# RWKV time mixes on one core: 32x32 blocks instead of 16x16 blocks inverted on VectorE

## Chip, core and metric

The kernel runs on one NeuronCore of a Trainium2 chip. The metric is the device time of one execution in microseconds (us), from the first to the last instruction of the core. A profiled execution gives the trace. Engines are named as in the trace: PE is TensorE (PEld its weight loads), DVE is VectorE, ACT is ScalarE, POOL is GpSimd, SP is SyncE; "ACTq" and the like are instructions by which an engine's queue issues a DMA.

## What is computed

A network of four blocks and a fifth of another kind, for one sequence of 256 tokens, width 1024. Each of the four has a mixer between two feed-forward layers; the mixers are an RWKV-7 time mix, a Mamba-2 mix, a windowed attention and again an RWKV-7 time mix. Only the two time mixes are touched (j = 0 and j = 1 in the code; mix 0 and mix 1 below). Their core, for 16 heads of 64 channels:

```python
def step(state, inp):                      # state 64 x 64 per head
    r_t, w_t, k_t, v_t, kk_t, a_t = inp
    sa = einsum('bhvk,bhk->bhv', state, -kk_t)
    state = (state * w_t[:, :, None, :]
             + sa[..., None] * (kk_t * a_t)[:, :, None, :]
             + v_t[..., None] * k_t[:, :, None, :])
    return state, einsum('bhvk,bhk->bhv', state, r_t)
_, y = lax.scan(step, state0, (r, decay, k, v, kk, a))
y = (y - mean(y)) * rsqrt(var(y) + eps) * ln_w + ln_b      # per head
out = ((y + sum(r * k * r_k) * v) * g) @ w_o
```

r, k, v and the low-rank w, a, g (in mix 1 also the share of the first mix's v, `v_first`) are projections of six mixes of the input with its predecessor.

## The kernel before, in words

The scan over 256 tokens is done in two chunks of 128 (`b`), each for two halves of the heads (`hf`, 8 heads each): four units u = 0 to 3, `RwUnit`. Within a unit the term `sa` needs, per head, the inverse of a unit lower triangular 128 x 128 matrix made of the products of a and kk. It is built up in levels.

**The 16x16 blocks.** While TensorE works on the projections, `near(u)` in `rw_products` multiplies a by kk for all units. ScalarE's `near_read(u)` (L2063) copies the 32x32 diagonal blocks to SBUF, and VectorE's `choose(u)` (L2349) keeps of them the 16x16 blocks of the diagonal. ScalarE issues four DMAs in turn through the DRAM tensor `near_rows`, each waiting for the one ahead with `moved(step)`: `low_out` (L2079), `low_in` (L2084), `base_out` (L2087) and `base_in` (L2091). The way in spreads the 256 blocks (16 heads, 16 blocks each over the 256 tokens) over 64 partitions, four to a partition. VectorE's `invert` (L2361) then eliminates in 15 steps of two instructions (L2368, L2370). The way out and in again leaves the inverses in `wkv_base`, in the layout of the units.

```python
for c in range(15):
    n, w = c + 1, 15 - c
    own.of(v.tensor_tensor(step, low[...c, n:16]..., x[...0:n, c:n]..., mult))
    own.of(v.tensor_tensor(x[:, :, 0:n, n:16], x[:, :, 0:n, n:16], step, sub))
```

**The levels.** In the recurrence VectorE's `open_y` (L2435) puts a unit's inverses on the diagonal of y, `turn_y` (L2446) transposes them to x. TensorE's `level16` (L1825), `x32`, `y32` join 16 to 32 (each a `half_products` of 16 products of 64x64 blocks, answered by a step of VectorE of the same name), `level32` and `y64` join 32 to 64. From 64 to 128 there is no inverse; `upper`, `across` and `lower` solve in two halves instead, with a copy by ScalarE behind `upper` and behind `lower` (`upper_read`, `lower_read`), and a VectorE addition behind `across`.

**The order of the work** is written out by hand, one list for each engine, in `rw_products` (TensorE, loop from L1966), `rw_act` (ScalarE) and `rw_vector` (VectorE, loop from L2551). Engines meet through semaphores: `at(name, c)` waits for a unit's step. The loop is a pipeline over n = 1 to 3, called pass 1 to 3 below: `head`, unit n, is brought up to its keys while `tail`, unit n - 1, goes through `rest` (L1874), `first_outs` (L1891), `upper`, `across`, `lower` and `state_and_out` (L1922), and unit n - 2 is normalised (VectorE `centre`, `variance`, `normed`; TensorE `turn_out`; ScalarE `out_read`, L2211; VectorE `gated`, L2523). In pass 3 TensorE calls `early_outputs(0)` (L1931) behind `state_and_out`; its first wait is for `rw_gated` of units 0 and 1. All other output products stand behind it.

**What runs beside.** `beside(n)` on VectorE takes n chunks of the modulation sums of a later layer (L524, 1.8 us each) in mix 0 alone; their DMAs (`ada_in`) come from POOL as buffers fall free. SP streams the weights. In the stretch ahead of the recurrence ScalarE reads the projections' tiles (`evacuate`, L2057): r, v, g1, g2. It may read g2 only when VectorE has ended `gate_mixes`, `bonus`, `beside(2)` and `scaled_both` (semaphore `rw_keys`, L2389), since g lies where e_out was. `near_again(0)` on TensorE waits for g2's reads. TensorE's g1 needs the gate mixes, which VectorE makes behind `invert`. In mix 1 ScalarE also issues the load of `v_first` (L2145) for VectorE's `mixed_values` (L2407).

## Time and profile before

| | us |
|---|---|
| three runs, median (lowest to highest) | 2961.02 (2960.65 to 2970.45) |
| the profiled execution | 2962.74 |
| its span in the trace | 2961.1 |
| PE busy | 2868.6, 97% |
| DVE busy | 2287.1, 77% |
| ACT busy | 1404.0, 47% |
| mean granted TensorE clock | 0.988 of full |

The profiled execution's own time stands 1.6 us above its span, and the median of the runs 1.7 us below that time. The shares are means over the whole network, most of it feed-forward layers; what a change in them is worth is read from their own stretches. A timeline row gives the start in us from the span's start, the us it lasts, the engine, the line, the operation, the tiles written and read, shapes and the number of merged instructions; in brackets stands the engine's idle time before and who ended it. TensorE's fp32 products leave two records each.

### The profile page before, as it was taken

The numbers are of one execution on the slowest core, as the hardware profiler recorded it, in microseconds if no ns is written. First come the engines' busy times: TensorE is split into PE (matmuls) and PEld (weight loads), VectorE is DVE, ScalarE is ACT, GpSimd is POOL, SyncE is SP. The second block draws the span as 40 slices with busy tenths as digits, with TensorE's granted clock in tenths as the row PEclk, the third lists the DMA queues.
The fourth block names the chain that finished last, engine by engine and source line by source line (L and its number), as shares of the span: only waits on it lengthen the run. The fifth ranks groups of instructions, "written<-read, shape, count | busy, mean of one in ns | idle before, by whom it ended". The sixth has DMA issues, their size and how long they took to land. (4 is left out here: it accounts for less than half of the span.)

```text
span 2961.1 us, 49642 instructions
## 1 busy us (share of the span) xinstructions
PE 2868.6 (97%) x19878; PEld 2544.1 (86%) x19878; DVE 2287.1 (77%) x3308; ACT 1404.0 (47%) x2292; POOL 97.2 (3%) x187
## 2 busy tenths in 40 slices
PE   7999999999999999999999999999999999999998
PEld 6887898888888888888886888887898889989887
DVE  6987678898878958888867888887555868775785
ACT  4544224445545835545444555544224544565553
POOL 0000000000000000000000000000000000000000
PEclk9999999999999999999999999999999999999999
DMA  8684527685666436676764666672403553443453
GB/s 350 256 311 177 200 87 264 248 334 210 250 239 241 164 141 259 239 266 241 272 250 153 245 242 266 239 283 96 173 2 129 192 192 131 174 166 144 175 185 130
DMA packets 75367, 615.48 MB, mean 208 GB/s; under 512 B 12096, under 2 KB 12304, under 8 KB 37520
## 3 DMA queue, kind: packets, MB, share of 16 engines
q1 hardware_dynamic: 42768, 459.36, 41.5%
q0 software_dynamic: 26352, 144.59, 13.1%
q10 hardware_dynamic: 6032, 8.47, 0.9%
q8 instruction: 158, 2.59, 0.3%
q14 instruction: 57, 0.47, 0.0%
HBM read 609.21 MB, written 3.18 MB: 207 GB/s over the span
## 5 line engine op out<-in xcount | busy, mean ns | idle before, releaser
L1076 ACT ACTIVATE unit_high<-weights 128x1024 fp32r<-128x1024 f32 x576 | 609.7, 1060 | 622.5 <-PE psum L1145 331.4
L1087 DVE TENSOR_TENSOR unit_low<-weights,unit_high 128x1024 fp32r<-128x1024 f32 x576 | 703.0, 1222 | 145.6 <-ACT unit_high L1076 145.2
L1141 PE MATMUL psum<-h_part,unit_high 128*128 128x512 f32 x3024 | 767.8, 393 | 5.0 <-DVE h_part L998 5.0
L1141 PEld LDWEIGHTS psum<-h_part,unit_high 128*128 128x128 f32 x3024 | 541.3, 189 | 105.0 <-DVE h_part L998 5.5
L1145 PEld LDWEIGHTS psum<-h_part,unit_low 128*128 128x128 f32 x3024 | 416.2, 190 | 30.8
L1145 PE MATMUL psum<-h_part,unit_low 128*128 128x256 f32 x3024 | 431.8, 282 | 0.0
L333 PE MATMUL psum<-in_part,w_part 128*128 128x256 f32 x2784 | 357.2, 289 | 17.7 <-issue 8.0
L333 PEld LDWEIGHTS psum<-in_part,w_part 128*128 128x128 f32 x2784 | 345.4, 195 | 24.9 <-issue 19.1
L1162 PE MATMUL psum<-hidden,unit_high 128*128 128x512 f32 x1386 | 349.1, 393 | 0.0
L524 DVE SCALAR_TENSOR_TENSOR ada_sum<-ada_in,c_act,ada_sum 128x1536 f32<-128x1536 f32 x154 | 278.6, 1812 | 36.2 <-DMA ada_in<-in_ada_w 36.2
L1282 DVE TENSOR_REDUCE arena<-psum 128x256 f32<-128x512 f32 x378 | 259.9, 688 | 48.8 <-PE psum L1145 38.3
L1162 PEld LDWEIGHTS psum<-hidden,unit_high 128*128 128x128 f32 x1386 | 249.4, 189 | 44.1
L333 PE MATMUL psum<-arena,weights 128*128 128x256 f32 (+4 forms) x1360 | 264.1, 369 | 7.3 <-DVE arena L2243 5.5
L333 PEld LDWEIGHTS psum<-arena,weights 128*128 128x128 f32 (+3 forms) x1360 | 214.9, 188 | 52.7 <-issue 20.3
L1169 PEld LDWEIGHTS psum<-hidden,unit_low 128*128 128x128 f32 x1584 | 215.3, 191 | 13.4
L1440 DVE TENSOR_TENSOR w_part<-weights,w_part 128x1024 fp32r<-128x1024 f32 x144 | 174.8, 1220 | 67.1 <-ACT w_part L1434 66.0
L1169 PE MATMUL psum<-hidden,unit_low 128*128 128x256 f32 x1584 | 221.9, 283 | 0.0
L333 PE MATMUL psum<-arena 64*64 64x64 f32 (+5 forms) x2752 | 174.3, 252 | 5.2 <-DVE arena L2973 4.7
L333 PEld LDWEIGHTS psum<-arena 64*64 64x64 f32 (+3 forms) x2752 | 144.2, 149 | 29.5 <-issue 16.1
L1434 ACT ACTIVATE w_part<-weights 128x1024 fp32r<-128x1024 f32 x144 | 150.7, 1049 | 16.6 <-PE psum L333 16.6
L1247 ACT ACTIVATE hidden<-arena 128x256 fp32r<-128x256 f32 x198 | 83.0, 419 | 112.1 <-DVE arena L1349 91.8
L508 POOL DMA_DIRECT2D ada_in<-in_ada_w x130 | 68.6, 528 | 1423.4 <-DVE ada_sum L524 1083.7
(335 smaller groups left out, 2725.1 us busy)
## 6 DMA issues: line engine op xcount, KB each, us to landing
weights<-in_weights SPq DMA_DIRECT2D x290, 1536.0 KB, 6.5
ada_in<-in_ada_w POOLq DMA_DIRECT2D x182, 768.0 KB, 5.9
raw<-acum_rows ACTq DMA_DIRECT2D x8, 512.0 KB, 4.8
consts<-in_consts POOLq DMA_DIRECT2D x1, 1414.0 KB, 12.9
x<-in_x SPq DMA_DIRECT2D x1, 1024.0 KB, 9.1
v_first<-arena ACTq DMA_DIRECT2D x1, 1024.0 KB, 5.5
arena<-v_first ACTq DMA_DIRECT2D x1, 1024.0 KB, 4.7
weights<-in_weights SPq DMA_DIRECT2D x1, 512.0 KB, 5.6
```

Source lines behind the costliest of these rows:

```text
L333: ins = self.k.nc.tensor.matmul(out, lhsT=w, rhs=x, start=start, stop=stop, is_transpose=turn)
L524: ins = k.nc.vector.scalar_tensor_tensor(out, buf, c, out, ALU.mult, ALU.add)
L1076: k.nc.scalar.activation(k.unit_part[0][:, n % UNIT_RING], w, ACT.Copy).then_inc(k.sem["unit_high"], 1)
L1087: k.nc.vector.tensor_tensor(k.unit_part[1][:, n % UNIT_RING], w, k.unit_part[0][:, n % UNIT_RING].bitcast(FP32), ALU.subtract).then_inc(k. ...
L1141: mm(k.psum[:, 2 * (j % 2) + half, :].rearrange("p (i t) -> p i t", i=2), lhsT=part(2 * j + half, 0, t), rhs=k.h_parts[:, :, t], start=t = ...
L1145: ins = mm(k.psum[:, 2 * (j % 2) + half, 0:T], lhsT=part(2 * j + half, 1, t), rhs=k.h_part[0][:, t], start=False, stop=t == KT - 1, skip_g ...
L1162: mm(k.psum[:, out_bank(d), :].rearrange("p (i t) -> p i t", i=2), lhsT=w, rhs=x, start=f == 0, stop=f == FT - 1, skip_group_check=True)
L1169: ins = mm(k.psum[:, out_bank(d), 0:T], lhsT=part(UNITS_UP + v, 1, b), rhs=k.hidden_part[f][:, 0], start=False, stop=f == FT - 1, skip_gro ...
L1247: k.nc.scalar.activation(k.hidden_part[j][:, 0], k.hidden[:, j % RING], ACT.Copy)\
L1282: v.tensor_reduce(to[:, j % RING], k.psum[:, 2 * (j % 2) + half, :].rearrange("p (i t) -> p t i", i=2), AX.X, ALU.add).then_inc(k.sem["gat ...
L1434: self.k.nc.scalar.activation(self.k.w_part[0][:, m % RING], w, ACT.Copy).then_inc(self.k.sem["w_high"], 1)
L1440: self.k.nc.vector.tensor_tensor(self.k.w_part[1][:, m % RING], self.weights(m)[1], self.k.w_part[0][:, m % RING].bitcast(FP32), ALU.subtr ...
```

## The change

VectorE inverts 32x32 blocks, one to a partition on all 128, in 31 steps of two instructions, instead of 16x16 blocks, four to a partition on 64, in 15. So `choose` and the level from 16 to 32 (`level16`, `x32`, `y32`, on TensorE and VectorE) are gone. `near_read` writes `near_t` directly. The way out is two DMAs, `low_out(0)` and `low_out(1)`, of half the units each; `near_rows` holds pieces of 32 numbers (128 bytes) where it held rows of 64 (256 bytes), and twice the data in all. `base_out` moves from behind v tile 2 to behind v tile 6, `base_in` from behind tile 3 to behind all of them, and it is two DMAs, one for unit 0 and one (semaphore `base_moved`) for the rest, into `raw` instead of `wkv_base`. The orders in the recurrence change as shown: the receptances stand ahead of y64 in unit 0; in the loop `rest` comes first, y64 moves ahead of `upper`, the keys ahead of `state_and_out`, `lower` between their halves; on VectorE `gated` moves behind `centre`, `open_y` and `turn_y` around the keys, and the chunks of `beside` are dealt out anew (three ahead of the inversion instead of one, two in each pass instead of two or three).

```diff
@@ -1600,14 +1594,13 @@
-        self.step = k.small[0:64, 192:448]
-        self.base = k.wkv_base[:, :].rearrange("p (m u t) -> p u m t", u=UNITS, m=8)
-        self.near_q = [cut(26 + i / 4, 256).rearrange("p (m t) -> p m t", m=8) for i in range(2)]
-        self.near_t = cut(26.5, 512).rearrange("p (m u t) -> p m u t", u=UNITS, m=8)
-        self.low = k.raw_flat[0:64, 0:1024].rearrange("p (s u t) -> p u s t", s=16, u=UNITS)
-        self.inverse = k.raw_flat[0:64, 1024:2048].rearrange("p (s u t) -> p u s t", s=16, u=UNITS)
+        self.step = k.small[:, 192:448]
+        self.near_t = cut(26, 1024).rearrange("p (u m t) -> p u m t", u=UNITS, m=8)
+        self.low = k.raw_flat[:, 0:1024].rearrange("p (s t) -> p s t", s=32)
+        self.inverse = k.raw_flat[:, 1024:2048].rearrange("p (s t) -> p s t", s=32)
         self.inverse_diagonal = bass.AP(tensor=k.raw_flat.tensor, offset=k.raw_flat.offset + 1024,
-                                        ap=[[KT * (T + 1), 64], [16 * UNITS + 1, 16], [16, UNITS]])
+                                        ap=[[KT * (T + 1), P], [33, 32]])
+        self.base = k.raw_flat[:, 0:1024].rearrange("p (u m t) -> p u m t", u=UNITS, m=8)
 
         self.vt = cut(0, 2048).rearrange("p (b n c) -> p b n c", b=2, n=KT)
...
@@ -1822,33 +1815,21 @@
-    def level16(c):
+    def level32(c):
         at("wk_am", c)
         at("wk_x_read", c)
         half_products(c, 0, 0, half_of_near(c), z.x[c.hf], s["wk_lx"])
 
-    def x32(c):
-        at("wk_t", c, 0, 2)
-        half_products(c, 0, 1, half_of(z.y[c.hf]), z.t[c.hf], s["wk_x32"])
-
-    def y32(c):
+    def receptances(c):
         if c.b:
             pe.wait_ge(s["wk_out_read"], UNITS * j + c.u - 1)
-        half_products(c, 1, 0, half_of(z.t[c.hf]), z.y[c.hf], s["wk_y32"])
-
-    def level32(c):
-        at("wk_x32_read", c)
-        half_products(c, 0, 0, half_of_near(c), z.x[c.hf], s["wk_lx"])
-
-    def receptances(c):
-        at("wk_y", c, 0, 2)
         for p in range(4):
             for i in range(2):
                 mm(c.pair(1)[:, 4 * i + p], z.a[z.rows(i), 4 * c.hf + p, z.now(c.b)],
                    z.r[z.rows(i), 4 * c.hf + p, z.now(c.b)], True, True, s["wk_ra"] if p == 3 and i else None)
 
     def y64(c):
-        at("wk_t", c, 1, 2)
+        at("wk_t", c)
         half_products(c, 0, 1, half_of(z.t[c.hf]), z.y[c.hf], s["wk_y64"])
 
...
@@ -1952,53 +1933,43 @@
-    level16(head)
     turn_values(0)
     turn_values(1)
-    x32(head)
-    y32(head)
     level32(head)
     turn_ended(0)
+    receptances(head)
     y64(head)
-    receptances(head)
     keys(head, lambda: turn_ended(1))
     pe.wait_ge(s["rw_turned_read"], 2 * (j + 1))
     near_again(units[1])
     for n in range(1, UNITS):
         head, tail = units[n], units[n - 1]
-        if n == 1:
-            rest(tail)
-        level16(head)
         with_mod = n == UNITS - 1 and j == 0
         if with_mod:
             at("wk_rk_read", tail, 0, 2)
             mod_sums(k, pe, pr, 2, range(6))
-        if n > 1:
-            rest(tail)
+        rest(tail)
+        level32(head)
         if with_mod:
             pe.wait_ge(s["mod_rows_read"], 3)
         first_outs(tail)
+        y64(head)
         upper(tail)
         if with_mod:
             turn_mod_rows(k, pe, pr, 2)
         if n >= 2:
             turn_out(units[n - 2])
-        x32(head)
         across(tail)
         if with_mod:
             pe.wait_ge(s["mod_ready"], 3)
-        y32(head)
-        lower(tail)
-        level32(head)
+        receptances(head)
+        keys(head, lambda: lower(tail))
         state_and_out(tail)
-        y64(head)
-        receptances(head)
         if n + 1 < UNITS:
             pe.wait_ge(s["wk_sa_read"], 2 * (UNITS * j + n))
             near_again(units[n + 1])
         else:
             early_outputs(0)
-        keys(head)
     tail = units[3]
     early_outputs(1)
     rest(tail)
...
@@ -2062,35 +2033,36 @@
 
-    by_row = near_rows.rearrange("m (c x) y -> (c x) m y", c=8)
-    by_block = near_rows.rearrange("m (c x) y -> (m c) (x y)", c=8)
+    by_row = near_rows.rearrange("n p t -> p n t")
+    by_block = near_rows.rearrange("n (c x) t -> (n c) (x t)", c=4)
 
     def moved(step):
-        act.wait_ge(s["near_moved"], 64 * j + 16 * step)
-
-    def low_out():
-        act.wait_ge(s["near_chosen"], UNITS * (j + 1))
-        act.dma_start(by_row, z.near_t.rearrange("p m u t -> p m (u t)")).then_inc(s["near_moved"], 16)
+        act.wait_ge(s["near_moved"], 80 * j + 16 * step)
+
+    def low_out(b):
+        act.wait_ge(s["wk_near_read"], UNITS * j + 2 * b + 2)
+        act.dma_start(by_row[:, 16 * b:16 * b + 16], z.near_t[:, 2 * b:2 * b + 2].rearrange("p u m t -> p (u m) t"))\
+            .then_inc(s["near_moved"], 16)
 
     def low_in():
-        moved(1)
-        act.dma_start(k.raw_flat[0:64, 0:1024], by_block).then_inc(s["near_moved"], 16)
+        moved(2)
+        act.dma_start(k.raw_flat[:, 0:1024], by_block).then_inc(s["near_moved"], 16)
 
     def base_out():
         act.wait_ge(s["wk_base"], j + 1)
-        act.dma_start(by_block, k.raw_flat[0:64, 1024:2048]).then_inc(s["near_moved"], 16)
+        act.dma_start(by_block, k.raw_flat[:, 1024:2048]).then_inc(s["near_moved"], 16)
 
     def base_in():
-        moved(3)
-        act.dma_start(k.wkv_base[:, :].rearrange("p (m x) -> p m x", m=8), by_row).then_inc(s["near_moved"], 16)
+        moved(4)
+        for first, end, signal in ((0, 1, "near_moved"), (1, UNITS, "base_moved")):
+            act.dma_start(z.base[:, first:end].rearrange("p u m t -> p (u m) t"), by_row[:, 8 * first:8 * end])\
+                .then_inc(s[signal], 16)
 
     picks = k.const("ident").rearrange("p (g n) -> p g n", g=4)
     rows = z.norm_rows.rearrange("p (r g h c) -> p r g h c", r=2, g=4, h=2)
...
@@ -2123,19 +2095,19 @@
         if m == 3:
+            low_out(0)
             near_read(2)
             near_read(3)
         if m == 4:
-            low_out()
+            low_out(1)
         if m == 5:
             low_in()
     act.wait_ge(s["rw_keys"], 3 * j + 1)
     for m in range(KT):
         evacuate("v", m, z.v[:, m], f.Copy)
-        if m == 2:
+        if m == 6:
             base_out()
-        if m == 3:
-            base_in()
+    base_in()
...
@@ -2346,28 +2318,20 @@
-    def choose(u):
-        dve.wait_ge(s["wk_near_read"], UNITS * j + u + 1)
-        even, odd = (k.const("halves16")[:, i:i + 1] for i in range(2))
-        q = z.near_q[u % 2]
-        own.of(v.tensor_scalar(z.near_t[:, :, u], q[:, :, 0:16], even, None, mult))
-        v.scalar_tensor_tensor(z.near_t[:, :, u], q[:, :, 16:32], odd, z.near_t[:, :, u], mult, add)\
-            .then_inc(s["near_chosen"], 1)
-
...
     def invert():
         own.wait()
-        dve.wait_ge(s["near_moved"], 64 * j + 32)
+        dve.wait_ge(s["near_moved"], 80 * j + 48)
         x, low = z.inverse, z.low
-        for c in range(15):
-            n, w = c + 1, 15 - c
-            step = z.step[:, 0:UNITS * n * w].rearrange("p (u r c) -> p u r c", u=UNITS, r=n)
-            own.of(v.tensor_tensor(step, low[:, :, c, n:16].unsqueeze(2).to_broadcast([64, UNITS, n, w]),
-                                   x[:, :, 0:n, c:n].to_broadcast([64, UNITS, n, w]), mult))
-            own.of(v.tensor_tensor(x[:, :, 0:n, n:16], x[:, :, 0:n, n:16], step, sub))
+        for c in range(31):
+            n, w = c + 1, 31 - c
+            step = z.step[:, 0:n * w].rearrange("p (r c) -> p r c", r=n)
+            own.of(v.tensor_tensor(step, low[:, c, n:32].unsqueeze(1).to_broadcast([P, n, w]),
+                                   x[:, 0:n, c:n].to_broadcast([P, n, w]), mult))
+            own.of(v.tensor_tensor(x[:, 0:n, n:32], x[:, 0:n, n:32], step, sub))
         v.tensor_copy(k.small[:, 101:102], k.const("eps")).then_inc(s["wk_base"], 1)
...
@@ -2388,13 +2352,9 @@
-    choose(0)
-    choose(1)
     value_mixes()
-    choose(2)
-    choose(3)
     open_inverse()
-    beside()
+    beside(3)
     invert()
     gate_mixes()
     bonus()
...
@@ -2435,11 +2395,14 @@
     def open_y(c):
         if c.b:
             dve.wait_ge(s["wk_sa"], 2 * (UNITS * j + c.u - 1))
-        dve.wait_ge(s["near_moved"], 64 * (j + 1))
-        same = k.const("same16_half").rearrange("p (c t) -> p c t", t=16).unsqueeze(1).to_broadcast([P, 4, 4, 16])
+        if c.u:
+            dve.wait_ge(s["base_moved"], 16 * (j + 1))
+        else:
+            dve.wait_ge(s["near_moved"], 80 * (j + 1))
+        same = k.const("same32_half").rearrange("p (c t) -> p c t", t=32).unsqueeze(1).to_broadcast([P, 4, 2, 32])
...
@@ -2483,7 +2432,7 @@
 
     def y64(c):
         at("wk_y64", c)
-        at("wk_y", c, 0, 2)
+        at("wk_open", c)
         v.tensor_tensor(by_half(z.y[c.hf]), by_half(z.y[c.hf]), c.halves(0, 1), add).then_inc(s["wk_y"], 1)
...
@@ -2529,58 +2478,46 @@
     projected("g1", 1)
-    open_y(head)
-    turn_y(head)
     if j:
         mixed_values(0)
         mixed_values(1)
     ended()
     values(0)
     values(1)
-    level16(head)
+    open_y(head)
+    turn_y(head)
+    level32(head)
+    receptances(head)
+    y64(head)
+    open_y(chunks[1])
     beside()
-    x32(head)
-    y32(head)
-    level32(head)
-    open_y(chunks[1])
-    y64(head)
+    keys(head, 0)
     turn_y(chunks[1])
-    receptances(head)
-    keys(head, 0)
     keys(head, 1)
     for n in range(1, UNITS):
         head, tail = chunks[n], chunks[n - 1]
         if n == UNITS - 1 and j == 0:
             mod_rows(k, dve, 2)
-        level16(head)
+        level32(head)
         if n >= 2:
             variance(chunks[n - 2])
-            beside()
             normed(chunks[n - 2])
-        else:
-            beside()
         if n == UNITS - 1 and j == 0:
             mod_columns(k, dve, own, 2)
-        x32(head)
+        y64(head)
+        beside()
         across(tail)
-        y32(head)
-        if n == 2:
-            beside()
-        level32(head)
+        receptances(head)
+        if n + 1 < UNITS:
+            open_y(chunks[n + 1])
+        keys(head, 0)
+        keys(head, 1)
+        if n + 1 < UNITS:
+            turn_y(chunks[n + 1])
+        centre(tail)
         if n >= 2:
             gated(chunks[n - 2])
-        else:
-            beside()
-        if n + 1 < UNITS:
-            open_y(chunks[n + 1])
         beside()
-        y64(head)
-        if n + 1 < UNITS:
-            turn_y(chunks[n + 1])
-        receptances(head)
-        keys(head, 0)
-        keys(head, 1)
-        centre(tail)
     variance(chunks[2])
     normed(chunks[2])
     beside(3)
```

## Rows read from the trace of the kernel before

**Rows 1.** The page, part 1: busy us (share of the span) x instructions.
```profile
PE 2868.6 (97%) x19878; PEld 2544.1 (86%) x19878; DVE 2287.1 (77%) x3308; ACT 1404.0 (47%) x2292; POOL 97.2 (3%) x187
```

**Rows 2.** Stretches: us; PE, PEld, DVE, ACT, POOL busy (x); clock, DMA, GB/s.
```profile
372.77:393.28 20.51, 19.93 (x368) 18.36 (x368) 14.16 (x18) 3.76 (x6) 1.58 (x3) 1.00 0.34 117
...
2179.81:2202.54 22.73, 22.06 (x341) 20.46 (x341) 13.26 (x23) 6.80 (x12) 0.00 (x0) 0.85 0.01 2
```

**Rows 3.** Timeline of PE, recurrence: start, us, what, count [idle before <-releaser].
```profile
354.43 1.16 PE L333 MATMUL psum<-arena 64*128 64x128 f32 x16
...
362.15 3.08 PE L333 MATMUL psum<-arena 64*64 64x64 f32 x96
...
372.77 2.00 PE L1874 MATMUL psum<-arena 128*128 128x64 f32 x16 [0.50 <-DVE arena L2493]
...
422.17 0.63 PE L333 MATMUL psum<-consts,arena 128*128 128x128 f32 x4
...
2202.54 2.00 PE L1874 MATMUL psum<-arena 128*128 128x64 f32 x16 [0.64 <-DVE arena L2493]
```

**Rows 4.** Timeline of ACT and its DMA queue, mix 0.
```profile
304.99 0.40 ACTq L2081 DMA_DIRECT2D near_rows<-arena  x1
...
341.95 0.38 ACT L2057 ACTIVATE arena<-psum 128x256 f32<-128x256 f32 x1 [3.07 <-PE psum L333]
...
352.01 1.25 ACT L2057 ACTIVATE arena<-psum 128x256 f32<-128x256 f32 x4 [2.77 <-PE psum L333]
...
378.88 0.59 ACT L2187 ACTIVATE arena<-psum 64x512 f32<-64x512 f32 x1 [3.48 <-PE psum L333]
...
422.84 1.50 ACT L2211 ACTIVATE arena<-psum,params 128x128 f32<-128x128 f32 x4 [0.22 <-PE psum L333]
```

**Rows 5.** Timeline of DVE, mix 0: centre (L2507 to L2509), gated (L2527).
```profile
393.15 0.68 DVE L2507 TENSOR_REDUCE small<-psum 128x8 f32<-128x512 f32 x1
...
394.07 0.69 DVE L2509 TENSOR_TENSOR arena<-psum,small 128x512 f32<-128x512 f32 x1
...
405.86 0.69 DVE L2527 TENSOR_TENSOR arena<-arena 128x512 f32<-128x512 f32 x1
```

**Rows 6.** Timeline of DVE, mix 0: the inversion and the end of scaled_both.
```profile
315.41 0.21 DVE L2368 TENSOR_TENSOR small<-raw 64x60 f32<-64x60 f32 x1 [7.46 <-DMA raw<-near_rows]
315.66 0.21 DVE L2370 TENSOR_TENSOR raw<-raw,small 64x60 f32<-64x60 f32 x1
...
320.56 0.42 DVE L2368 TENSOR_TENSOR small<-raw 64x256 f32<-64x256 f32 x1
321.01 0.42 DVE L2370 TENSOR_TENSOR raw<-raw,small 64x256 f32<-64x256 f32 x1
...
326.69 0.15 DVE L2371 COPY small<-consts 128x1 f32<-128x1 f32 x1
...
341.07 0.15 DVE L2389 COPY small<-consts 128x1 f32<-128x1 f32 x1
```

**Rows 7.** DMA by stretch: issues (KB, us to landing); one queue's packets; v_first's load.
```profile
near_rows<-arena ACTq DMA_DIRECT2D x1, 256.0 KB, 7.1
...
raw<-near_rows ACTq DMA_DIRECT2D x1, 256.0 KB, 3.2
...
wkv_base<-near_rows ACTq DMA_DIRECT2D x1, 256.0 KB, 2.8
...
q10 hardware_dynamic: 1040, 0.26, 32.0%
...
arena<-v_first ACTq DMA_DIRECT2D x1, 1024.0 KB, 4.7
```

**Rows 8.** Timeline of mix 1, DVE and ACT's DMA queue.
```profile
2095.81 0.21 DVE L2368 TENSOR_TENSOR small<-raw 64x60 f32<-64x60 f32 x1 [9.11 <-DMA raw<-near_rows]
...
2125.86 0.34 ACTq L2145 DMA_DIRECT2D arena<-v_first  x1
...
2135.66 1.23 DVE L2407 TENSOR_TENSOR arena<-arena 128x1024 f32<-128x1024 f32 x1 [1.39 <-ACT arena L2057]
```

41 lines of the change are left out of this document (11 added, 30 removed).

## Prediction

> **What bounds the kernel now.** I read the page first: TensorE (PE) is busy for 97% of the span [rows 1], so a change pays only where it shortens TensorE's own stream or one of its waits. The change touches the two RWKV time mixes (one ends near 476 us of the span, one near 2263), and in each of them two stretches. The first is the projection stretch. TensorE streams weight tiles there, while VectorE (DVE) inverts blocks; the inversion matters only if something behind it comes late. The second is the recurrence, four units in a software pipeline. The busy times by stretch show two passes of its loop: 20.51 us with TensorE busy 19.93, and 22.73 with 22.06 [rows 2], while VectorE has room (14.16 and 13.26). So the loop is bound by TensorE's order of small products; the timeline shows its parts [rows 3].
>
> **What leaves the loop.** Per unit three half_products of 16 small products go (level16, x32, y32). The trace has exactly three such groups back to back, 96 records in 3.08 us [rows 3]: 1.03 us each. Units 1 to 3 lie in the loop, so 9 groups, **9.3 us per mix**. With them go three VectorE steps of 0.7 us per unit, and their waits. TensorE also waits for VectorE ahead of `rest`, 0.50 us in mix 0 and 0.64 in mix 1 [rows 3], in two or three passes of each; I take 0.8 us for mix 0 and 1.8 for mix 1. These vanish, because by my count VectorE ends keys(head, 1) over 1 us before TensorE is back at `rest`.
>
> **What the new order exposes.** The removed groups also covered latencies.
> - across(tail) now follows upper(tail) at once. It needs ScalarE's read of upper, 0.59 us [rows 4], plus some 0.2 us of signalling: 0.8 us in pass 1. In passes 2 and 3 turn_out, 0.63 us [rows 3], lies between, which leaves 0.2 each. Together 1.2.
> - receptances(head) of units 2 and 3 waits for out_read, 1.50 us on ScalarE [rows 4], behind upper's read and covered by across alone (some 1.05): 0.5 each, together 1.0.
> - gated(1) moves. It was ahead of receptances and keys on VectorE in pass 3; now it stands behind centre(2), which waits for state_and_out(2). But TensorE's early_outputs(0), right behind state_and_out(2), waits for rw_gated of units 0 and 1. So TensorE idles for centre, three instructions from 393.15 to 394.76, and gated, two of 0.69 [rows 5]: 1.6 + 1.4 + 0.1 = **3.1 us**. Nothing covers it, since all the output products are queued behind.
>
> Sum of the loop: mix 0 -9.3 - 0.8 + 1.2 + 1.0 + 3.1 = -4.8; mix 1 one more, -5.8.
>
> **The inversion.** Neighbouring starts give the price of one step: 60 elements 0.25 us, 256 elements 0.45 us [rows 6], so 0.189 us fixed and 1.02 ns per element. Before: 30 instructions, 5,440 elements, 11.2 us (the trace has 11.28). After: 62 instructions; the sum of n(32 - n) over n is 5,456, twice that 10,912 elements: 11.7 + 11.1 = **22.8 us**. That it now spans 128 partitions costs nothing in the formula; a 128-row step elsewhere (0.69 us for 512 elements [rows 5]) lies on the same line. *The Trainium skill's page "VectorE: DVE Perf Modes", section "The TRN2 errata", gives (N+151)/0.96 ns for such an fp32 step and asks for tiles of at least 512 elements, so it speaks against more and smaller steps; by it the sum would be 21.1 us.* I take the rows, as they hold the issue gap too.
>
> **When it starts and who waits.** The four choose steps go. beside(3) instead of beside(1) fills the wait for the round trip, which is 7.46 us now [rows 6]. The way out is now two transfers of 2,048 pieces of 128 B, where it was one of 1,024 of 256 B. The second one still leaves at about 305.0 [rows 4]. A thousand such pieces landed in 7.1 us beside a weight load and in 2.8 alone; 1,040 packets took 32.0% of 16 engines over 3.6 us, 18 ns each [rows 7]. If a piece costs the same at half its size, 1,024 more add 1.2 us; beside the extra ada_in load I take 9. The way in doubles to 512 KB, 3.2 us [rows 7] plus about 1. The inversion starts near 319 and ends near 342 instead of 326.69. The last v tile is read at 341.95 [rows 4], so g1's first mix is late by under 1 us, and that wait runs beside the longer chain: VectorE needs from 326.69 to 341.07 [rows 6] for gate mixes, bonus, two chunks and the last scaling, 14.4 us, so rw_keys comes at 356.4 instead of 341.1. ScalarE then starts g2's reads 4.4 us after 352.01 [rows 4], and near_again(0) moves from 354.43 [rows 3] to 357.9. From there: bonus sums to 361.6, values to 362.4 or so (I allow 363.5), open_y and turn_y (1.4, formerly in idle time) to 364.9, then level32, y64, keys with one chunk between. `rest` of pass 1 starts near 375.9 instead of 372.77: **+3.1 us in mix 0**, in which the shorter chain has already paid for part of the delay.
>
> **Mix 1** has no ada chunks. The inversion started at 2095.81 and would now start near 2098 and end near 2121, 5 us ahead of the first use of its mixes. The base goes back beside v tiles. But base_in is now 4,096 pieces in two transfers, and ScalarE issues v_first's load (2125.86) behind it, which mixed_values needs at 2135.66 [rows 8]. By 18 ns a piece 4.6 us of engine time go ahead of it, and moved(4) holds ScalarE up some 1.5 us: the load itself takes 4.7 [rows 7], so 5.1 us of room were there, and the two together with the weight load beside them overdraw it by 1.3 (bounds: 0, and 16 as in rival 2). The chain without level16, x32, y32 gains 0.5. Head: **+0.8**. base_in's first part is due only at open_y(0), some 14 us or more after the issue.
>
> **Sum:** mix 0 +3.1 - 4.8 = -1.7; mix 1 +0.8 - 5.8 = -5.0; together -6.7 us. On the profiled execution's 2962.74 us (span 2961.1) that is 2956.0; the median of the runs is 2961.02, 1.7 lower, so I forecast **2954.3 us**.
>
> **Rivals.**
> 1. *The waits that I add don't appear*: the new order hides them and v_first comes in time. Then mix 0 is -10.1 + 3.1 and mix 1 is -11.1 - 0.5: -18.6, 2942.4 us. For it: ScalarE's reads are short. Against it: early_outputs(0) and gated(1) are in the text of the order, no estimate.
> 2. *The small pieces decide, and it gets slower.* If a transfer's time goes by its number of pieces at the contended row, 7.1 us per 1,024 [rows 7], the way out takes 14 us and the way in 6.4. In mix 0 the inversion ends at 348.4, rw_keys at 362.8: +9.5 at the head. In mix 1 it ends at 2129, g1's mixes are 3 us late, base_out takes 11 and base_in 11 (4 x 2.8, alone) or more, and v_first lands at 2152 or later: +16. Total +9.5 - 4.8 + 16 - 5.8 = +15, 2976 us. It turns slower from the point where pieces of 128 B cost some three times 18 ns. Against it: that 7.1 us was shared with 1.5 MB of weights. *The page "DMA: Bandwidth & Descriptors" of the Trainium skill, section "Specifications", says that pieces below 512 B are read, modified and written; it bears on both sizes, and no row here has 128 B pieces.*
> 3. *The clock.* In one pass of mix 1 the granted clock averages 0.85 over 22.73 us [rows 2]: 2 x 0.15 x 22.73 = 6.8 us at the lower of the two levels, 1.2 GHz, which costs up to 3.4 us. TensorE would wait in new places (3 us ahead of near_again(0) in mix 0, 3.1 in each early_outputs). Two more such stretches: -6.7 + 6.8, 2961 us.
>
> **Chances.** Forecast 0.54, rival 1 0.22, rival 2 0.12, rival 3 0.12. A measurement of this kernel can tell about 0.5%, 14.8 us, from no change. Rival 1 is beyond it on the fast side, rival 2 on the slow side, the other two within: faster 0.22, same 0.66, slower 0.12. The range takes in rival 1 and rival 3 and the bounds of the DMA terms up to +16 on the forecast: 2942 to 2970 us.
>
> **What would show it.** In the timeline of the changed kernel: 62 steps of inversion in 22.8 us, ending near 342 and 2121; TensorE at `rest` of pass 1 near 375.9 and 2160.3; passes 1 and 2 of 17.2 to 18 us; a wait of TensorE of about 3.1 us on gated (VectorE) ahead of early_outputs in each mix; near_rows transfers of 8 to 9 us. I am wrong if the pass is still 20 us (the groups were not on the path), if the 3.1 us wait is absent, or if TensorE waits in the projections for gate mixes.

## The result, and the profile after

The changed kernel takes **2980.07 us** (median of 6 runs, 2974.66 to 2983.74), the kernel before in runs on the same chip 2961.37 (6 runs, 2959.40 to 2970.45). The ratio is 1.0053, with a 95% interval of 1.0037 to 1.0068. (The ratios in this document are drawn from all the runs and are not quotients of two medians; that quotient is 1.0063 here.) I had forecast 2954.3 in a range of 2942 to 2970; it is slower, and outside the range. The profiled execution took 2981.36 us with a span of 2979.7, 18.6 above the span before.

The page of the changed kernel, part 1:

```profile
PE 2863.9 (96%) x19110; PEld 2536.6 (85%) x19110; DVE 2289.9 (77%) x3332; ACT 1404.0 (47%) x2292; POOL 97.1 (3%) x187
```

Against [rows 1] TensorE has 768 instructions fewer, as the change says (three groups of 32 records for each of eight units), but only 4.7 us less busy time, although at 1.03 us a group 24.7 us of work went. Busy time that stays while work goes points to a slower clock, and the mean granted clock is 0.983 of full, before 0.988.

The timeline of PE, where [rows 3] has the same points of before (the product at L328, `rest` at L1855):

```profile
344.40 9.75 PE L328 MATMUL psum<-arena,weights 128*128 128x256 f32 x32 [5.06 <-DVE arena L2215]
...
359.75 1.16 PE L328 MATMUL psum<-arena 64*128 64x128 f32 x16
...
377.43 2.00 PE L1855 MATMUL psum<-arena 128*128 128x64 f32 x16 [1.28 <-DVE arena L2442]
394.44 2.00 PE L1855 MATMUL psum<-arena 128*128 128x64 f32 x16
416.33 2.79 PE L328 MATMUL psum<-ada_sum,consts 128*32 128x128 f32 x48 [4.39 <-issue]
419.05 3.68 PE L1855 MATMUL psum<-arena 128*128 128x64 f32 x16
...
455.98 1.90 PE L1855 MATMUL psum<-arena 128*128 128x64 f32 x16
```

Pass 1 (377.43 to 394.44) is 17.0 us where it was 20.5, just under the 17.2 to 18 forecast. Then comes the thing that the prediction does not have: at 416.33 TensorE stands 4.39 us ahead of `mod_sums`, the products that sum up the modulation for a later layer, called ahead of pass 3's `rest`. Pass 3 itself, from 419.05, ends at 455.98: 36.9 us, before 22.4 (414.92 to 437.33). The stretches of that part, columns as in [rows 2]:

```profile
377.43:394.44 17.01, 16.33 (x241) 14.85 (x241) 9.10 (x13) 2.17 (x4) 0.53 (x1) 1.00 0.19 71
406.50:414.50 8.00, 5.44 (x76) 4.67 (x74) 6.59 (x13) 2.63 (x4) 0.00 (x0) 1.00 0.05 19
414.50:441.80 27.30, 25.47 (x236) 23.79 (x238) 7.68 (x14) 3.00 (x7) 1.05 (x2) 0.50 0.17 52
```

From 414.5, two and a half microseconds into the wait, the granted clock is 0.50 for 27.3 us, the lower level, 1.2 GHz (called half clock below). TensorE is busy 25.5 us of it.

Why the wait: `mod_sums` needs all 16 chunks of its layer (`ada_summed`, L637). The trace names no releaser for the wait, but the timeline of DVE shows the last chunk at the end of pass 2, behind centre and gated, and it ends at 416.23, 0.1 us before the sums begin:

```profile
412.49 0.69 DVE L2458 TENSOR_TENSOR arena<-psum,small 128x512 f32<-128x512 f32 x1
413.10 0.68 DVE L2475 TENSOR_TENSOR arena<-arena 128x512 f32<-128x512 f32 x1
413.81 0.69 DVE L2476 TENSOR_TENSOR arena<-arena 128x512 f32<-128x512 f32 x1
414.42 1.81 DVE L518 SCALAR_TENSOR_TENSOR ada_sum<-ada_in,c_act,ada_sum 128x1536 f32<-128x1536 f32 x1
```

In the kernel before, the same chunk (L524) began at 407.14, in the middle of the pass, and was done at 408.95, and TensorE reached the sums at 413.47 with no wait. The chunk and the sums there, DVE and PE:

```profile
407.14 1.81 DVE L524 SCALAR_TENSOR_TENSOR ada_sum<-ada_in,c_act,ada_sum 128x1536 f32<-128x1536 f32 x1
```

```profile
413.47 1.52 PE L333 MATMUL psum<-ada_sum,consts 128*32 128x128 f32 x48
```

The head of mix 0, ACT's queue and DVE, where [rows 4] and [rows 6] have before:

```profile
301.63 0.37 ACTq L2050 DMA_DIRECT2D near_rows<-arena  x1
...
314.07 0.34 ACTq L2055 DMA_DIRECT2D raw<-near_rows  x1
```

```profile
303.42 1.82 DVE L518 SCALAR_TENSOR_TENSOR ada_sum<-ada_in,c_act,ada_sum 128x1536 f32<-128x1536 f32 x1 [3.38 <-DMA ada_in<-in_ada_w]
...
343.71 0.15 DVE L2335 COPY small<-consts 128x1 f32<-128x1 f32 x1
343.78 3.25 DVE L2215 SCALAR_TENSOR_TENSOR arena<-arena,params 128x256 f32<-128x256 f32 x8
```

The second store landed 12.4 us after its issue. Beside it ran, in part, three ada_in loads (issued at 298.61, 300.34 and 305.54) and two weight loads (301.88 and 312.24); in the kernel before, beside the one store, it was one of each. The load landed 6.2 us after its own issue. The inversion ran from 320.3 to 343.7, 23.4 us. This execution reached the near products 2.65 us earlier than the one before, so against its own start the inversion ended 4.4 us later than forecast. The wait of 5.06 us ahead of g1, shown above at 344.40, is the result, and half clock falls there too, for 6.8 us from 342.8. Mix 1, ACT's queue and PE:

```profile
2114.03 0.34 ACTq L2055 DMA_DIRECT2D raw<-near_rows  x1
2140.96 0.34 ACTq L2059 DMA_DIRECT2D near_rows<-raw  x1
2146.81 1.01 ACTq L2064 DMA_DIRECT2D raw<-near_rows  x2
2147.90 6.62 ACTq L2117 DMA_DIRECT2D arena<-v_first  x1
```

```profile
2156.61 3.71 PE L328 MATMUL psum<-arena,weights 32*128 32x256 f32 x32 [2.54 <-ACT arena L2028]
...
2237.42 2.93 PE L328 MATMUL psum<-arena,weights 128*128 128x128 f32 x12 [3.04 <-DVE arena L2476]
```

The issue of v_first's load alone took ScalarE 6.62 us, before 0.34 [rows 8]. The 3.04 us ahead of `early_outputs(0)` are the wait on gated that was forecast.

Where the 18.6 us come from: mix 0 from the near products to the residual (294.31 to 474.39 before, 291.66 to 493.63 after) is 21.9 us longer and mix 1 about 2.7 shorter; the stretches ahead of and between the mixes, which the change does not touch, are 2.65 shorter and 2.1 longer in this one execution. Mix 0 as a whole, before and then after:

```profile
294.31:474.39 180.08, 177.51 (x2033) 160.81 (x2033) 122.37 (x187) 42.52 (x93) 10.03 (x19) 1.00 0.45 156
...
291.66:493.63 201.97, 185.10 (x1653) 165.75 (x1653) 123.40 (x198) 42.61 (x93) 10.03 (x19) 0.90 0.43 144
```

TensorE is busy 7.6 us more, although twelve groups, some 12.4 us, are gone: so half clock is some 20 us, by this one execution. It is idle for 16.9 us and not 2.6, 14.3 more. 20 and 14.3 less the 12.4 are the 21.9 us.

### The profile page after: what moved, and what is told of

Read it like the earlier page. It is cut to its first block and busy times, and to the rows that moved or that the text cites. A ratio compares the mean times of both kernels' runs of the same rounds, so it can differ in the third digit from the quotient of the medians.

```text
span 2979.7 us, 48113 instructions
## 1 busy us (share of the span) xinstructions
PE 2863.9 (96%) x19110; PEld 2536.6 (85%) x19110; DVE 2289.9 (77%) x3332; ACT 1404.0 (47%) x2292; POOL 97.1 (3%) x187
## 5 line engine op out<-in xcount | busy, mean ns | idle before, releaser
L1139 PEld LDWEIGHTS psum<-h_part,unit_low 128*128 128x128 f32 x3024 | 416.2, 190 | 30.7
L328 PE MATMUL psum<-in_part,w_part 128*128 128x256 f32 x2784 | 358.1, 289 | 19.7 <-issue 8.1
L328 PEld LDWEIGHTS psum<-in_part,w_part 128*128 128x128 f32 x2784 | 346.6, 195 | 26.8 <-issue 21.3
L328 PE MATMUL psum<-arena,weights 128*128 128x256 f32 (+4 forms) x1360 | 272.2, 377 | 19.4 <-DVE arena L2215 9.5
L328 PEld LDWEIGHTS psum<-arena,weights 128*128 128x128 f32 (+3 forms) x1360 | 222.2, 194 | 65.4 <-issue 25.1
L328 PE MATMUL psum<-arena 64*64 64x64 f32 (+6 forms) x1984 | 156.9, 269 | 10.0 <-DVE arena L2910 4.7
L328 PEld LDWEIGHTS psum<-arena 64*64 64x64 f32 (+3 forms) x1984 | 125.3, 159 | 35.6 <-issue 16.4
```

Of the source, the lines that this page charges most:

```text
L328: ins = self.k.nc.tensor.matmul(out, lhsT=w, rhs=x, start=start, stop=stop, is_transpose=turn)
L1139: ins = mm(k.psum[:, 2 * (j % 2) + half, 0:T], lhsT=part(2 * j + half, 1, t), rhs=k.h_part[0][:, t], start=False, stop=t == KT - 1, skip_g ...
```

## Experiments

Each kernel is the changed one with the edit shown, except where said. The first number is the median, then its ratio to the kernel before on the same chip. The changed kernel stands at 1.0053. The sets ran on different chips, where the median of the kernel before was between 2961.37 and 2966.78 us, so ratios are compared and not medians. All of them are within 1% of the kernel before; what counts is whether their intervals meet.

### First set: one suspected cost each

**chunk_early**: each pass's last chunk right behind the keys, ahead of centre and gated.

```diff
         keys(head, 1)
+        beside()
         if n + 1 < UNITS:
             turn_y(chunks[n + 1])
...
-        beside()
     variance(chunks[2])
```

> The changed kernel, with VectorE's last chunk of each loop pass moved from the pass's end (behind centre and gated) to right behind keys(head, 1). In the changed kernel TensorE idles 4.39 us ahead of the modulation sums in pass 3 of mix 0, until that chunk (414.42 to 416.23) is done, and from about then the granted clock is halved for 27.3 us. Theory A: the halved stretch follows from this wait. Then the wait goes (4.4 us) and with it the halved stretch (pass 3 from rest to early_outputs took 30.4 us in mix 0 and 20.4 in mix 1, so 10 us): about -14 us against the changed kernel's 2980, 2966. Theory B: the low clock has another cause (the small products of the recurrence alone). Then the wait goes and the halved stretch stays: -4.4 us, 2976.

2967.52 us (2964.17 to 2975.97), 1.0013 (1.0002 to 1.0023): by the ratios 12 us below the changed kernel, give or take some 5 by the two intervals. Its timeline of PE:

```profile
412.50 1.52 PE L328 MATMUL psum<-ada_sum,consts 128*32 128x128 f32 x48
...
436.52 3.78 PE L328 MATMUL psum<-arena,weights 128*128 128x128 f32 x16 [3.24 <-DVE arena L2476]
```

The last chunk now ends at 412.27, just ahead of the sums. The wait and the long stretch at half clock are gone, and `early_outputs(0)` comes at 436.5 and not at 449.4. One wait of 4.4 us cost 12 to 13. Short half-clock stretches of 3.4 and 6.8 us remain in pass 3. The profiled execution was the slowest of the ten, though, and its span (2974.3) is only 5.4 us below the changed kernel's: its mean granted clock is 0.982 over the whole network, so other stretches ran at half clock outside the pass, one of them of 6.8 us at 483.7. That the time falls by more than the wait rests on the ten runs and on the pass.

**gated_early**: in pass 3 VectorE takes gated(1) right behind the receptances.

```diff
         if n + 1 < UNITS:
             open_y(chunks[n + 1])
+        else:
+            gated(chunks[n - 2])
...
-        if n >= 2:
+        if n >= 2 and n + 1 < UNITS:
             gated(chunks[n - 2])
```

> The changed kernel with gated(1) of pass 3 moved from behind centre(2) to right behind receptances on VectorE, where the kernel before has it roughly. Theory A: TensorE's 3.04 us waits ahead of early_outputs(0), one in each mix, are this placement alone: both go, nothing else takes their place, -6 us: 2974 (and up to 3 us more if the halved clock behind that wait in mix 1 goes with it). Theory B: TensorE then waits for something else at that place (weights, the keys' reads): less than 2 us.

2969.85 us (2966.80 to 2971.10), 1.0023 (1.0013 to 1.0032). Both waits of 3.04 us go. That is 6 us, and 9 are gained by the ratios. The 3 above are within the intervals, but two short half-clock stretches that stood at those waits in the changed kernel (6.8 us from 448.7, 3.4 us from 2237.2) are missing too. The sums still wait 4.39 us, and the clock is still 0.50 over 27.3 us from 415.5.

**chunks_wait**: no chunk, and so no new ada_in load, until both stores of near_rows have landed.

```diff
     open_inverse()
+    dve.wait_ge(s["near_moved"], 80 * j + 32)
     beside(3)
```

> The changed kernel, but VectorE waits for both near_rows stores before it takes the three chunks ahead of the inversion, so that the ada_in loads which these chunks release no longer run beside the stores. Theory A: those loads made the second store of mix 0 take 12.4 us (7.95 in mix 1, which has no chunks). Then it lands in about 8 us, the inversion starts near 316 instead of 320.3, TensorE's wait for the gate mixes ahead of g1 falls from 5.06 to under 1.5 us, and the halved clock stretch behind it goes too: -4 to -7 us, 2973 to 2976. Theory B: the 2,048 pieces of 128 B are slow by themselves there: the store stays over 11 us and the total at 2980 or, as the chunks come later, slightly above.

2977.59 us (2969.80 to 2984.62), 1.0047 (1.0029 to 1.0064). The second store lands in 7.4 us instead of 12.4, now with no ada_in load beside it: those loads were what slowed it. The load lands in 3.4 instead of 6.2, between two weight loads and not beside one. But the time is hardly touched. The third chunk now waits for its own load and holds the inversion, and behind g1, where TensorE waits 2.3 us instead of 5.1, it waits anew:

```profile
344.22 7.15 PE L328 MATMUL psum<-arena,weights 128*128 128x256 f32 x32 [2.34 <-DVE arena L2215]
351.84 5.21 PE L328 MATMUL psum<-arena,weights 128*128 128x256 f32 x32 [0.47 <-ACT arena L2028]
359.36 1.79 PE L328 MATMUL psum<-arena 64*128 64x128 f32 x16 [2.31 <-ACT arena L2028]
...
378.65 2.30 PE L1855 MATMUL psum<-arena 128*128 128x64 f32 x16 [1.28 <-DVE arena L2443]
...
424.93 2.79 PE L328 MATMUL psum<-ada_sum,consts 128*32 128x128 f32 x48 [4.39 <-issue]
```

The same trace holds something that the account of the clock has to fit. The sums wait 4.39 us as in the changed kernel, but the half clock behind that wait lasts 3.4 us, and `rest` to `rest` of pass 3 (427.64 to 453.77) takes 26.1 us, not 36.9. But 17.1 us at half clock stand in pass 1, from 380.2 on, where the changed kernel ran at full clock:

```profile
380.30:397.20 16.90, 16.22 (x148) 14.73 (x148) 5.02 (x5) 1.19 (x2) 0.53 (x1) 0.50 0.13 48
```

The wait nearest ahead of it is the 1.28 us at 378.65, and the changed kernel has that one too.

**vfirst_first**: in mix 1 ScalarE issues v_first's load ahead of base_in.

```diff
-    base_in()
     if j == 0:
+        base_in()
...
         act.dma_start(z.v_first, v_first)...
+        base_in()
```

> The changed kernel; in mix 1 alone ScalarE issues the load of v_first ahead of the two base_in DMAs instead of behind them. Theory A: the 4,096 small pieces of base_in fill the queue, so that v_first's issue holds ScalarE for 6.62 us (0.34 in the kernel before) and its data come late; VectorE waits 7.17 us for them. Then v_first's issue takes about 0.35 us, VectorE's first use is no longer held by the DMA, rest of pass 1 comes some 2 us earlier relative to the start of the mix, and the total falls by about 2 us. Theory B: the queue or the weights delay it whatever the order: no change in mix 1.

2976.70 us (2964.16 to 2982.49), 1.0038 (1.0021 to 1.0055), not apart from the changed kernel by its time. The trace tells more: the issue takes 0.33 us again, the 2.54 us wait is 0.47, and pass 1's `rest` comes 2.1 us earlier after the start of mix 1's projections, 0.4 earlier than in the kernel before.

```profile
2148.12 0.33 ACTq L2117 DMA_DIRECT2D arena<-v_first  x1
2148.49 1.08 ACTq L2064 DMA_DIRECT2D raw<-near_rows  x2
```

So what I had priced as engine time of the pieces is, for the larger part, time for which the issuing queue is held.

### Second set: do the gains add, and has it to do with the blocks?

**early_pair**, chunk_early and gated_early together:

> The changed kernel with two of the moves tried so far: pass 2's last conditioning chunk right behind the second keys of that pass, and pass 3's gated step right behind its receptances. Theory A (the wait of the modulation sums for the 16th chunk, and the wait of early_outputs(0) for the gated step, are separate costs): their gains add, 12.5 us and about 10 us off the changed kernel's 2980, so 2956 to 2960, a ratio of 0.997 to 0.999 to the kernel before; no wait ahead of the modulation sums, none of 3.04 us at early_outputs(0). Theory B (both are one cost, since either takes away the half-clock stretches behind them): together no more than the larger, 2966 to 2968, ratio 1.001 to 1.002.

2955.29 us (2951.62 to 2960.18), **0.9971** (0.9960 to 0.9982). This is the 32x32 kernel with two VectorE steps moved, and it beats the kernel before by 9 us, 0.3%, clear of its interval. The gains add, within the intervals (0.0040 and 0.0030 off 1.0053 are 0.9983). Its recurrence, `rest` to `rest`, takes 57.0 us in mix 0 and 55.3 in mix 1:

```profile
378.67 2.00 PE L1855 MATMUL psum<-arena 128*128 128x64 f32 x16 [1.28 <-DVE arena L2442]
...
435.69 1.90 PE L1855 MATMUL psum<-arena 128*128 128x64 f32 x16
```

**before_late_chunk** is the other direction: the *kernel before*, 16x16 blocks, with nothing but this:

```diff
-        beside()
+        if n != 2:
+            beside()
         y64(head)
...
         centre(tail)
+        if n == 2:
+            beside()
```

> The kernel before, with one move: the last conditioning chunk of pass 2 of mix 0 is taken behind that pass's centre and not ahead of its y64. It has the same arithmetic and 16x16 blocks. Theory A (the loss in the changed kernel is the wait of the modulation sums for this chunk, with the half clock that follows it, and has nothing to do with the block size): the sums wait 2 to 5 us, a half-clock stretch follows, and the time is 6 to 13 us above the kernel before, ratio 1.002 to 1.0045. Rival (the long half-clock stretch comes from the power drawn around it in the new order, and the wait is its price only by chance): the sums wait 2 to 5 us, no stretch of more than 7 us follows, and the time is 0 to 5 us above, ratio 1.000 to 1.0017.

2972.75 us (2963.54 to 2980.98, ten runs), 1.0031 (1.0016 to 1.0046). The late chunk alone slows the kernel before by 8 to 9 us. But the runs lie far apart, and the profiled one was low (2965.75): the wait is 3.94 us and only 3.4 us at half clock follow, which is what the rival expected. Two more traces of it, from single runs, follow.

> The kernel before with the last chunk of pass 2 taken late, once more, for its trace: its ten runs fell apart into 2963.5 to 2965.8 and 2968.5 to 2981, and the one profiled was of the low ones, with a wait of 3.94 us and 3.4 us at half clock behind it. Theory A (what makes the high ones is a long half-clock stretch behind that wait): a run above 2970 shows a stretch of 15 us or more between the modulation sums and the last rest pass; one below 2967 shows none above 7 us. Rival: a high run has its added time elsewhere.

2966.35 us, again 3.4 us. Here a low run shows none above 7 us, as expected; it could not tell more.

> The kernel before with the late chunk, for its trace a third time: two profiled runs (2965.8 and 2966.4) showed a wait of 3.94 us and 3.4 us at half clock behind it. A run above 2970 shows a half-clock stretch of 15 us or more behind that wait, if a long stretch is what sets the high runs apart; a run above 2970 without one speaks against it.

2971.91 us, with a stretch of 20.5 us. The first trace, two stretches from the end of the wait on:

```profile
415.20:418.60 3.40, 3.40 (x53) 3.02 (x52) 0.82 (x3) 0.00 (x0) 0.53 (x1) 0.52 0.53 178
418.60:435.70 17.10, 17.10 (x283) 16.27 (x283) 9.46 (x17) 3.47 (x8) 1.06 (x2) 1.00 0.20 64
```

The third trace, from the same point:

```profile
415.40:435.90 20.50, 20.50 (x204) 19.20 (x198) 5.20 (x11) 2.88 (x7) 0.82 (x2) 0.50 0.22 78
```

And its timeline of PE, with the wait:

```profile
414.97 2.33 PE L333 MATMUL psum<-ada_sum,consts 128*32 128x128 f32 x48 [3.95 <-issue]
```

In the one, TensorE's `rest` to `rest` of pass 3 takes 22.9 us (417.67 to 440.59), in the other 30.7 (417.23 to 447.89). The same program, the same wait within 0.01 us, and a half-clock stretch of 3.4 or of 20.5. So the program does not set the length of the stretch. It is the same with the changed kernel's wait of 4.39 us: 27.3 us at half clock in the changed kernel, gated_early and vfirst_first, 3.4 in chunks_wait and in gates_first (third set). In chunks_wait and in all_four, below, a stretch of 17.1 us began where no new wait stands. What is shown is that the wait was there each time the long stretch stood at the sums, and that neither is there in the runs that take it away; that a wait alone opens such a stretch is not. Of the two explanations on record before the runs, the low traces look like the rival, the third and the median of the ten runs like theory A. My bound of 2970 fits, if narrowly, and it was set on other chips: on that of the third run the median of the kernel before was 2966.78. Runs of 2975 and more, of which this kernel had five, were not profiled, so what they have at the sums is not known.

**all_four**, the four edits of the first set, and **all_two_ahead**, the same with two chunks ahead of the inversion and the third behind the bonus products:

> The same four moves with three chunks ahead of the inversion. Theory A: the four gains add as ratios (0.0040, 0.0030, 0.0015 and 0.0006 off 1.0053), 0.9962, so 2951 to 2954; a wait of 2 to 2.5 us at g1 stays. Against it: the half-clock stretches move and the sum of single gains isn't reached, 2956 to 2962.

> All four moves (the two of the pair; mix 1's v_first load ahead of base_in; VectorE waits for both near_rows stores before its chunks ahead of the inversion), and only two chunks stand ahead of the inversion, the third behind the bonus products. Theory A (the second store shares the DMA engines with ada_in loads, and the third chunk then waits for its own load): second store lands in about 7.4 us as in the run with the wait, the inversion begins at most 17 us after near(0) closes instead of 20, the wait of TensorE at g1 falls from 5.06 us to under 1 us, and the time is 2950 to 2956, ratio 0.995 to 0.998. Rival (the time lost at g1 comes back at near_again, which waits for work of ScalarE, as the run with the wait showed with 2.31 us): g1's wait goes but near_again's grows, and the time is the pair's less some 2 us for mix 1, 2955 to 2958.

all_four: 2957.87 us (2944.11 to 2965.39), 0.9973 (0.9957 to 0.9989), no better than the pair, as the case against it said. In its trace the wait of 2.3 us at near_again stays, with 3.4 us at half clock behind it, and 17.1 us at half clock come from 379.4 on, 21 us after that wait and at the same place as in chunks_wait. all_two_ahead: 2963.62 us (2957.72 to 2968.33), 0.9997 (0.9985 to 1.0008), a miss. The inversion began 11.4 us behind the second store's issue, not 18.7, and the wait at g1 went, and near_again waited 11.89 us, because the chunk put behind the bonus waited for its load:

```profile
362.20 1.82 DVE L518 SCALAR_TENSOR_TENSOR ada_sum<-ada_in,c_act,ada_sum 128x1536 f32<-128x1536 f32 x1 [9.69 <-DMA ada_in<-in_ada_w]
```

### Third set: the wait at g1

VectorE idles for 15 us ahead of the inversion, and the gate mixes, for which g1 waits, need nothing from it. **gates_first** moves them there in mix 0; **three_moves** is the pair with it, **four_moves** has vfirst_first's edit too.

```diff
     beside(3)
+    if j == 0:
+        gate_mixes()
     invert()
-    gate_mixes()
+    if j:
+        gate_mixes()
```

> The changed kernel with one move: in mix 0 VectorE makes the gate mixes ahead of the inversion, in its idle stretch of 15 us before the base is read, and not behind it. Theory A (the changed kernel loses 5.06 us at g1 because the gate mixes stand behind an inversion that ends 4.4 us after v): the wait at g1 goes, the inversion still begins near 26 us after near(0), near_again follows the v, g1 and g2 projections with at most 1 us of wait, and the time falls by 5 us, 7 to 9 us if the half-clock stretch of 6.8 us behind that wait goes too: 2971 to 2975, ratio 1.0022 to 1.0038 to the kernel before. The wait of the modulation sums for the chunk stays, as does the long half-clock stretch. Rival (what is saved at g1 is waited at near_again, since scaled_both still ends behind the inversion): g1's wait goes and near_again waits 2 us or more, 2976 to 2979.

> The pair (2955.3, ratio 0.9971) with the gate mixes of mix 0 ahead of the inversion. Theory A: 4.4 us of waiting at g1 goes, and 0 to 3.4 us of the half clock behind it: 2947 to 2951, ratio 0.9945 to 0.9957. Rival (near_again takes over the wait): 2952 to 2956.

> The three moves and, in mix 1, the v_first load ahead of base_in. The single run gave 2.1 us ahead of rest pass 1 of mix 1, so 2945 to 2949, ratio 0.9938 to 0.995. Against it: base_in's pieces land 9 to 11 us after their issue instead of 6 and delay the first rows of the recurrence, no gain over the three moves.

Measured: 2979.02 us (1.0072, 1.0053 to 1.0091, four runs), 2960.47 (0.9998, 0.9988 to 1.0008), 2959.36 (0.9989, 0.9978 to 1.0001). All three missed their theory: three_moves is 5 us *above* the pair, and four_moves is no gain clear of three_moves, as the case against it said, though in its trace pass 1's `rest` of mix 1 does come 2.3 us earlier. The wait at g1 is gone, and one of 14.45 us stands behind it, for ScalarE's read (14.33 in gates_first, 14.79 in four_moves). Three_moves, ACT and its queue:

```profile
344.14 0.34 ACTq L2059 DMA_DIRECT2D near_rows<-raw  x1
344.53 0.38 ACT L2028 ACTIVATE arena<-psum 128x256 f32<-128x256 f32 x1 [7.73 <-DVE small L2335]
351.98 1.06 ACTq L2064 DMA_DIRECT2D raw<-near_rows  x2
353.08 6.07 ACTq L2113 DMA_DIRECT2D v_first<-arena  x1
359.19 1.28 ACT L2028 ACT_TABLE_LOAD   x1 [14.27 <-DMA raw<-near_rows]
360.48 0.66 ACT L2028 ACTIVATE arena<-psum 128x256 f32<-128x256 f32 x2
```

g1's reads are in one line behind base_in, which waits until base_out has landed, and behind the v_first store. In the changed kernel base_out landed 2.7 us after its issue and the store's issue took 1.94; here it is 7.8 and 6.07. The difference is what runs beside them. With TensorE not held up, SP issues the next 1.5 MB of weights at 343.89, on top of base_out, where in the changed kernel it came at 351.30; and two ada_in loads, issued at 349.30 and 351.03 (352.21 and 353.94 in the changed kernel), lie beside base_in and the store. So by these traces TensorE's stall at g1 had kept the DMA engines free for the base.

**three_and_reads** is three_moves with ScalarE's order changed in mix 0: v_first's store right behind base_out, base_in behind g1's reads.

```diff
-    base_in()
     if j == 0:
...
     else:
+        base_in()
...
     evacuate("g1", 1, ...)
+    if j == 0:
+        base_in()
```

> The three moves, and in mix 0 ScalarE stores v_first right behind base_out and issues base_in only behind the reads of g1. Theory A (in the three moves TensorE waited 14.45 us for g1's read on ScalarE, because that read stands behind base_in, which waits for base_out to land, and behind the v_first store, whose issue took 6.07 us behind base_in's small pieces): the store's issue takes under 1 us, TensorE's wait there falls below 3 us, and near_again is at most 4 us behind rw_keys' copy; rest pass 1 begins 5 to 9 us earlier, 2951 to 2956, ratio 0.9960 to 0.9985. Rival (base_out and base_in are slowed by the weight loads that now start earlier, and rest pass 1 waits for the base, whatever the order on ScalarE): a wait of 4 us or more for raw<-near_rows ahead of the first rows that read the base, 2957 to 2961, no gain over the three moves.

2953.95 us (2950.91 to 2963.78), **0.9964** (0.9948 to 0.9981). The store's issue takes 0.33 us, the wait of 14.45 us is 0.97, and near_again waits 4.11 us.

```profile
345.89 0.33 ACTq L2112 DMA_DIRECT2D v_first<-arena  x1
346.25 1.28 ACT L2028 ACT_TABLE_LOAD   x1 [0.39 <-ACT arena L2028]
347.55 0.66 ACT L2028 ACTIVATE arena<-psum 128x256 f32<-128x256 f32 x2
354.51 1.01 ACTq L2064 DMA_DIRECT2D raw<-near_rows  x2
```

Base_out still takes 9.4 us to land and the base itself 7 to 9, but nobody on the path waits for them. So the order on ScalarE was the cause of the loss in three_moves, whose interval does not meet this one, and the slow transfers counted through it. Against the pair (0.9971) the gain of 0.0007 is within the intervals: what is shown is the return from three_moves, not a step beyond the pair.

## Why the prediction was wrong, point by point

- **What leaves the loop, and the new order: right as far as it went.** Pass 1 takes 17.0 us in both mixes (17.2 to 18 forecast). The wait on gated ahead of `early_outputs(0)` is 3.04 us in each mix, forecast 3.1. Mix 1's recurrence is 5.2 us shorter (65.24 to 60.05), forecast 5.8.
- **The inversion: right.** 23.4 us for 22.8, 10 ns a step more than the price from the rows. *The formula of the Trainium skill's page "VectorE: DVE Perf Modes" ("The TRN2 errata") gave 21.1; the trace is 2.3 above it. For the length of a single step they agree (0.19 us for 31 elements, 0.42 for 256); the 2.3 us are some 37 ns from the end of each step to the start of the next.*
- **The step that failed: the list under "What the new order exposes" has no wait of the sums products.** The prediction took the chunks of `beside` as filler and, for the change, counted only how many stand ahead of the inversion and in the chain behind it. It put the wait for the last chunk of a set at nothing, without a reason. By the diff, pass 2's second chunk moves behind centre and gated, and the sums products of pass 3 wait for that very chunk: 4.39 us. The rows of before would have told it. There the chunk ended at 408.95 and TensorE came to the sums at 413.47: 4.5 us of slack. In the changed kernel the chunk ends 6.1 us later in the pass (21.8 us behind `rest` for 15.7), and TensorE, with three groups fewer on the way (x32, y32 and the next unit's level16), is there 2.7 us sooner (17.5 for 20.2). 4.5 - 6.1 - 2.7 is -4.3: the wait, as measured. chunk_early and before_late_chunk show this wait and its cause from both sides.
- **The clock: the forecast's sum has no term for it. The mechanism was rival 3's, its place and size were not.** I gave it two stretches like the one of 6.8 us at [rows 2], 3.4 us of cost each. At one wait stood 27.3 us, of which TensorE was busy 25.5, at half speed: up to 13 us. Another execution or another kernel with the same wait had 3.4 us there, so the size in one trace is partly chance. Mix 0's pass 2 and 3 together came out 17.5 us longer than before (44.05 to 61.54); 4.4 of it is the wait, 3.0 gated's, and most of the rest the clock.
- **The transfers: the size of a term.** I took 9 us for the second store "beside the extra ada_in load"; it took 12.4 in mix 0 beside three such loads in part (7.4 in chunks_wait with none) and 7.95 in mix 1, which has none. This put the inversion's end 4.4 us later, and the wait at g1 was 5.06 us, not under 1, with 6.8 us at half clock about it. Rival 2's price per piece did not come true; its direction did, in a small part.
- **v_first: the right place, the wrong reason.** I had it overdraw by 1.3 us through engine time of the pieces ahead. In fact ScalarE's queue stood 6.62 us in the issue itself. The head of mix 1 came out at +1.7 us, forecast +0.8.
- **The sum.** Forecast was a ratio of 0.9977, measured 1.0053, 22.5 us apart (26 by the medians). The missed wait with its clock is 12 of them (chunk_early, 1.0013; 15 by the medians). Of the other 11, the heads of the mixes are 5 by the traces (4.2 in mix 0, 1.0 in mix 1); the rest was not taken apart term by term. The two short half-clock stretches that go with gated's waits in gated_early suggest that clock beside waits that I had priced at their length alone is part of it. In the one trace mix 0, forecast 1.7 us shorter, is 21.9 longer: its groups save 12.4, but TensorE is idle 14.3 us more, of which the sums' wait, g1's and gated's are 12.5, and half clock costs some 20, for which the sum had no term.

## What to carry to other kernels

A filler that is moved or dealt out anew is work with a consumer: find who waits for the last one of each set, and what slack it had, before calling it free. Price a new wait of TensorE at its length, and leave room for what the clock may take beside it: here 4.4 us cost 12 in the changed kernel. In the kernel before, the wait of 3.9 us and the longer pass 3 together (22.4 us before, 22.9 and 30.7 with it) came to 4.5 us in one trace and 12.2 in another. One trace does not give that price. And where one engine both issues DMAs and reads PSUM, a wait or an issue that is slow stands in front of every read behind it, so a stall removed elsewhere may only uncover it.

## What the runs showed of the hardware that was not expected

- An issue of a 1 MB DMA on ScalarE's queue took 0.33 us, but 6.62 us when it followed base_in's 4,096 pieces of 128 bytes with a weight load beside them (mix 1), 6.07 with two ada_in loads there (three_moves, mix 0), and 1.94 with neither (mix 0). The engine did nothing else meanwhile. *The Trainium skill's page "DMA: Bandwidth & Descriptors", section "Issuing engines are not separate DMA queues", calls the time to initiate a DMA usually small relative to the DMA; here it was 6.62 of the 11.2 us from the issue's start to landing.*
- The same wait of 3.94 us in the same program was followed by 3.4 us at 1.2 GHz in two traces and by 20.5 us in a third. TensorE was busy throughout each stretch. A stretch of 17.1 us began in two other kernels (chunks_wait, all_four) where the 15 us ahead held only waits of 0.41, 0.84 and 1.28 us, which the changed kernel has at full clock. What decides place and length stays open. Moving the sums products behind `rest` on TensorE, which would take the wait away from the other side, was not tried.
- The store of 128-byte pieces landed in 12.4 us as the changed kernel has it, and in 7.4 when VectorE's chunks, which set off new ada_in loads, waited for it; base_out, 512 KB, took 2.7 us alone, 5.8 (mix 1) and 7.8 (three_moves) beside a weight load, and 9.4 beside a weight load and v_first's store.
